# Hybrid streaming encoder on one core: the streams' RoPE scores as one single-pass product of split keys and queries

## The reference, cut to what matters

```python
def mla_attend(q_lat, q_pe, ckv, kpe, q_pos, k_pos):
    s = einsum('bqhc,bkc->bhqk', q_lat, ckv) + einsum('bqhr,bkr->bhqk', q_pe, kpe)
    s = where(mask, s * MLA_SCALE, min)
    p = softmax(s, axis=-1)
    return einsum('bhqk,bkc->bqhc', p, ckv)
```

## Time and profile before

| | |
|---|---|
| median of 3 runs | 2976.04 us |
| the runs | 2971.38, 2976.04, 2981.77 |
| the profiled execution's own time | 2976.23 us |
| its span, first to last instruction | 2974.4 us |
| mean granted TensorE clock | 0.972 |
| TensorE matmul busy | 2803.0 us (94%) |
| VectorE busy | 1292.5 us (43%) |
| ScalarE busy | 883.6 us (30%) |
| GpSimd busy | 348.3 us (12%) |

### The profile page before, as it was taken

The page is one execution under the profiler, slowest core; times in us unless marked ns, Lnnn a source line. Parts: engine busy times, 40 slices in busy tenths (PEclk is TensorE's granted clock), DMA queues, the critical chain, the costliest instruction groups (busy, mean ns, idle before and its releaser), DMA issues.

```text
span 2974.4 us, 45234 instructions
## 1 busy us (share of the span) xinstructions
PE 2803.0 (94%) x18690; PEld 2663.0 (90%) x18690; DVE 1292.5 (43%) x1803; ACT 883.6 (30%) x1158; POOL 348.3 (12%) x310
## 2 busy tenths in 40 slices
PE   6999999998988999999999999999889799999997
PEld 6999999995667999999989999989766688999997
DVE  3332334546566533333363323354475656332334
ACT  4221223316422332122342212242363234221222
POOL 0110111002121111001101001110202210100110
PEclk8999999999988999999999999999999799999998
DMA  3222224210004222222222232233000142223222
GB/s 109 76 66 85 71 61 107 67 40 7 20 17 80 58 71 74 80 72 62 82 69 71 73 83 71 62 84 88 19 3 28 45 72 57 71 68 87 71 58 76
DMA packets 367380, 190.42 MB, mean 64 GB/s; under 512 B 36421, under 2 KB 363160, under 8 KB 367262
## 3 DMA queue, kind: packets, MB, share of 16 engines
q1 hardware_dynamic: 363262, 178.30, 22.5%
q0 software_dynamic: 4000, 10.47, 1.4%
HBM read 182.81 MB, written 5.93 MB: 63 GB/s over the span
## 4 chain that ended last, share of the span: by engine, by line
PE 85%; DVE 8%; ACT 3%; issue 3%; SPq 0%; DMA 0%; ACTq 0%; DVEq 0%; POOL 0%; POOLq 0%
PE ps L582 25%; PE ps L583 24%; PE ps L584 24%; PE ps L817 2%; ACT w L1234 1%; PE ps L826 1%; DVE w L1661 1%; PE ps L877 1%; PE ps L945 1%; PE ps L859 1%; DVE y L1750 1%; PE ps L923 1%; DVE at L1932 1%; PE ps L924 1%; PE ps L618 0%
## 5 line engine op out<-in xcount | busy, mean ns | idle before, releaser
L582 PE MATMUL ps<-xh,w 128*128 128x320 f32 x3456 | 1081.8, 313 | 44.6 <-DVE xl L1729 17.6
L583 PE MATMUL ps<-xl,w 128*128 128x320 f32 x3456 | 1075.8, 311 | 0.0
L584 PE MATMUL ps<-xh,w 128*128 128x320 f32 x3456 | 1075.8, 311 | 0.0
L582 PEld LDWEIGHTS ps<-xh,w 128*128 128x128 f32 x3456 | 656.0, 190 | 55.8 <-DVE xl L1729 24.3
L583 PEld LDWEIGHTS ps<-xl,w 128*128 128x128 f32 x3456 | 656.1, 190 | 0.3
L584 PEld LDWEIGHTS ps<-xh,w 128*128 128x128 f32 x3456 | 655.8, 190 | 0.0
L1661 DVE TENSOR_TENSOR w<-raw,w 128x2048 fp32r<-128x2048 f32 x180 | 420.5, 2336 | 420.5 <-ACT w L1234 420.5
L1234 ACT ACTIVATE w<-raw 128x2048 fp32r<-128x2048 f32 x181 | 345.2, 1907 | 452.3 <-PE ps L584 437.6
L582 PE MATMUL ps<-hh,w 128*128 128x320 f32 x1408 | 437.4, 311 | 1.0 <-DVE w L1661 1.0
L584 PE MATMUL ps<-hh,w 128*128 128x320 f32 x1408 | 435.1, 309 | 0.0
L583 PE MATMUL ps<-hl,w 128*128 128x320 f32 x1408 | 435.1, 309 | 0.0
(11 more groups left out here) (347 smaller groups left out, 2737.8 us busy)
## 6 DMA issues: line engine op xcount, KB each, us to landing
raw<-in_w_ffn_in_dram SPq DMA_DIRECT2D x178, 512.0 KB
raw<-in_w_ffn_out_dram SPq DMA_DIRECT2D x64, 384.0 KB
raw<-in_w_ffn_out_dram SPq DMA_DIRECT2D x64, 320.0 KB
raw<-in_w_in_dram SPq DMA_DIRECT2D x38, 512.0 KB
raw<-in_w_out_dram SPq DMA_DIRECT2D x16, 512.0 KB
out_dram<-xio SPq DMA_DIRECT2D x5, 512.0 KB, 2.6
xio<-in_x_prompt_dram SPq DMA_DIRECT2D x1, 2048.0 KB
y<-in_cache_ckv_dram POOLq DMA_DIRECT2D x8, 256.0 KB, 3.2
```

Source lines behind the costliest of these rows:

```text
L582: pe.matmul(out, wh, xh, start=first, stop=False)
L583: pe.matmul(out, wh, xl, start=False, stop=False)
L584: return pe.matmul(out, wl, xh, start=False, stop=last)
```

## The change

The three partial products of a split RoPE score, high by high, high by low and low by high, are laid below each other in the 128 contracted rows, so that one float32r product of 512 columns replaces the float32 product of L924. Rows 0 to 31 hold the queries' high part and the keys' high part; rows 32 to 63 the queries' high and the keys' low; rows 64 to 95 the queries' low and the keys' high; rows 96 to 127 are zero. ACT writes the keys' high part twice, DVE the low part. The unsplit queries go to QRAW, in rows 32 to 63 of the scratch tile UB, and are split once per layer. KPT lies where it lay, over GB. On ACT the first exponential now stands ahead of stream 1's keys, and TensorE's first `stream_transpose` gets three spins. Two semaphores (`setup_ps`, `y_stored`) are merged into others (`xio_ps`, `ml_stored`), with the thresholds moved along.

```diff
-    QPE = tile(s_w, "qpe", [P, NSEQ, H, TS])
+    QPE = tile(s_w, "qpe", [P, NSEQ, H, TS], F32R)
-    KN = tile(s_w, "kn", [ROPE, P])
+    KN = tile(s_w, "kn", [2 * ROPE, P])
+    QRAW = UB[ROPE:2 * ROPE, :, :].rearrange("p c t -> p (c t)")[:, 0:NSEQ * P].rearrange("p (b h t) -> p b h t", b=NSEQ, h=H)
+    rope_hi, rope_lo = event("rope_hi", NSEQ + 1), event("rope_lo", NSEQ + 1)
...
 TensorE, stream_keys
             if b:
                 pe.wait_ge(*ct_sb.nth(l, b - 1))
+                pe.wait_ge(*rope_lo.nth(l, b))
...
 TensorE, stream_scores
             pe.wait_ge(*ct_sb.nth(l, b))
+            pe.wait_ge(*rope_lo.nth(l, b + 1))
...
-            qn = QPE[0:ROPE, b, :, :].rearrange("c h t -> c (h t)")
+            qn = QRAW[:, b, :, :].rearrange("c h t -> c (h t)")
             pe.matmul(PS[:, 4, :], ql, CT[:, b % 2, :], start=True, stop=False)
             pe.matmul(PS[:, 4, :], qp, KPT[:, b % 2, 0:PAST], start=False, stop=True)
...
 TensorE, stream_transpose
             if b:
                 pe.wait_ge(*spt_sb.nth(l, b - 1))
-                held(pe)
-                spin(PS[:, 2, :], 1)
+            held(pe)
+            spin(PS[:, 2, :], 1 if b else 3)
             pe.wait_ge(*sp_sb.nth(l, b))
...
 ACT, latent_queries
-                run(QPE[0:ROPE, :, h, :], PS[0:ROPE, 2, P:2 * P].rearrange("p (b t) -> p b t", t=TS), ACT.Copy)\
+                run(QRAW[:, :, h, :], PS[0:ROPE, 2, P:2 * P].rearrange("p (b t) -> p b t", t=TS), ACT.Copy)\
...
 ACT, the loop over n
+                if n == NT - 2:
+                    run(QPE[ROPE:2 * ROPE, :, :, :], QRAW, ACT.Copy)
+                    run(QPE[0:ROPE, :, :, :], QRAW, ACT.Copy).then_inc(rope_hi.sem, 1)
...
 ACT, stream_keys
+                run(KPT[0:ROPE, b % 2, 0:PAST], PS[0:ROPE, 1, :], ACT.Copy).then_inc(rope_hi.sem, 1)
                 run(CT[:, b % 2, :], PS[:, 0, :], ACT.Copy)
-                run(KPT[0:ROPE, b % 2, 0:PAST], PS[0:ROPE, 1, :], ACT.Copy).then_inc(ct_sb.sem, 1)
+                act.wait_ge(*rope_hi.nth(l, b + 1))
+                run(KPT[2 * ROPE:3 * ROPE, b % 2, 0:PAST], KPT[0:ROPE, b % 2, 0:PAST].bitcast(F32), ACT.Copy)\
+                    .then_inc(ct_sb.sem, 1)
...
 ACT, the start of the streams
             pair_output(H // 2 - 1)
+            stream_exp(0)
             stream_keys(1)
-            stream_exp(0)
             stream_transposed(0)
...
 DVE, mla
-            V.memset(QPE[ROPE:64, :, :, :], 0.0)
-            V.memset(QPE[64:P, :, :, :], 0.0)
+            V.memset(QPE[3 * ROPE:P, :, :, :].bitcast(F32), 0.0)
...
                 if n == NT - 3:
-                    V.memset(KPT[ROPE:64, :, 0:PAST], 0.0)
-                    V.memset(KPT[64:P, :, 0:PAST], 0.0)
+                    V.memset(KPT[3 * ROPE:P, :, 0:PAST].bitcast(F32), 0.0)
+            dve.wait_ge(*rope_hi.nth(l, 0))
+            V.tensor_tensor(QPE[2 * ROPE:3 * ROPE, :, :, :], QRAW, QPE[ROPE:2 * ROPE, :, :, :].bitcast(F32), ALU.subtract)\
+                .then_inc(rope_lo.sem, 1)
             for n in range(NT - 3, NT):
                 normalise(n)
+
+            def stream_rope_low(b):
+                dve.wait_ge(*rope_hi.nth(l, b + 1))
+                V.tensor_tensor(KPT[ROPE:2 * ROPE, b % 2, 0:PAST], PS[0:ROPE, 1, :],
+                                KPT[0:ROPE, b % 2, 0:PAST].bitcast(F32), ALU.subtract).then_inc(rope_lo.sem, 1)
...
             dve.wait_ge(*pn_zero.nth(l, 0))
...
+            stream_rope_low(0)
             stream_maximum(0)
             level(0)
             stream_normalise(0)
             level(1)
+            stream_rope_low(1)
             stream_maximum(1)
...
                 for k in range(early):
+                    if k == early - 1 and b + 2 < NSEQ:
+                        stream_rope_low(b + 2)
                     level(m + k)
```

More of the change, by code:

```diff
@@ L182, in encoder @@
     tile(ctx, "w_rest", [P, P * 2])
+    s_w = ExitStack()
+    KPT = tile(s_w, "kpt", [P, 2, T], F32R)
+    s_w.close()
     GB = tile(ctx, "gb", [P, 2, T])
@@ L273, in encoder @@
     s_w.close()
-    ROPET, SWAP, PAIR, KPT = UB[NOPE:P, 0, :], UB[0:QK, 1, 0:P], UB[NOPE:P, 1, P:P + ROPE], GB
+    ROPET, SWAP, PAIR = UB[NOPE:P, 0, :], UB[0:QK, 1, 0:P], UB[NOPE:P, 1, P:P + ROPE]
+    QRAW = UB[ROPE:2 * ROPE, :, :].rearrange("p c t -> p (c t)")[:, 0:NSEQ * P].rearrange("p (b h t) -> p b h t", b=NSEQ, h=H)
     SC, DROP = PB[0:NSEQ * 3, 0, :], KPER[0:MH, :]
@@ L318, in encoder @@
     setup_in = sem("setup_in")
-    setup_ps, setup_sb = sem("setup_ps"), sem("setup_sb")
+    setup_sb = sem("setup_sb")
     xio_ps, xio_sb = sem("xio_ps"), sem("xio_sb")
@@ L393, in encoder @@
     ml_stored = sem("ml_stored")
-    y_stored = sem("y_stored")
     act_chain, dve_chain, pool_chain = sem("act_chain"), sem("dve_chain"), sem("pool_chain")
@@ L570, in _ @@
             dst = O["y_prompt"][0, t * P:(t + 1) * P, :] if t < PT_ else O["y_sample"].rearrange("b t f -> (b t) f")
-            sp.dma_start(dst, XIO[:, t, :]).then_inc(y_stored, 16)
-        sp.wait_ge(y_stored, 16 * TILES)
+            sp.dma_start(dst, XIO[:, t, :]).then_inc(ml_stored, 16)
         sp.wait_ge(stored, 16 * LAYER_STORES * LAYERS)
         sp.wait_ge(cn_stored, 32 * LAYERS)
-        sp.wait_ge(ml_stored, 256 * LAYERS)
+        sp.wait_ge(ml_stored, 256 * LAYERS + 16 * TILES)
     @block.tensor
@@ L925, in stream_scores @@
             pe.matmul(PS[:, 5, 0:TS], ql, CKVT[:, TP + b * TS:TP + (b + 1) * TS], start=True, stop=False)
-            pe.matmul(PS[:, 5, 0:TS], qn, KN[:, b * TS:(b + 1) * TS], start=False, stop=True)\
+            pe.matmul(PS[:, 5, 0:TS], qn, KN[ROPE:2 * ROPE, b * TS:(b + 1) * TS], start=False, stop=True)\
                 .then_inc(ss_ps.sem, 1)
@@ L1173, in _ @@
         pe.transpose(PS[:, 0, 96:146], PROW[0:50, 1, :], IDENT[0:50, 0:50])
-        pe.matmul(PS[:, 1, 0:LAYERS * DK], ONES[0:1, :], HROW[:, :], start=True, stop=True).then_inc(setup_ps, 1)
+        pe.matmul(PS[:, 1, 0:LAYERS * DK], ONES[0:1, :], HROW[:, :], start=True, stop=True).then_inc(xio_ps, 1)
         pe.wait_ge(setup_sb, 1)
@@ L1540, in mla @@
             stream_keys(0)
-            run(KN[:, :], KPER[NOPE:QK, TP:T], ACT.Copy).then_inc(kn_sb.sem, 1)
+            run(KN[ROPE:2 * ROPE, :], KPER[NOPE:QK, TP:T], ACT.Copy).then_inc(kn_sb.sem, 1)
             pair_output(H // 2 - 1)
+            stream_exp(0)
             stream_keys(1)
-            stream_exp(0)
             stream_transposed(0)
@@ L1627, in _ @@
         for c in range(KD):
-            act.wait_ge(xio_ps, c + 1)
+            act.wait_ge(xio_ps, c + 2)
             run(X[:, c, :], psf[:, (c % 4) * 1024:(c % 4) * 1024 + T], ACT.Copy).then_inc(xio_sb, 1)
@@ L1649, in _ @@
         for t in range(TILES):
-            act.wait_ge(xio_ps, KD + t + 1)
+            act.wait_ge(xio_ps, KD + t + 2)
             run(XIO[:, t, :], psf[:, (t % 4) * 1024:(t % 4) * 1024 + D], ACT.Copy).then_inc(xio_sb, 1)
@@ L2229, in _ @@
         V.memset(HB[:, 0, 4:6], 1.0).then_inc(dve_setup, 1)
-        dve.wait_ge(setup_ps, 1)
+        dve.wait_ge(xio_ps, 1)
         V.tensor_copy(PAR[:, :], PS[:, 0, 0:PAR.shape[1]]).then_inc(dve_setup, 1)
```

## The result

The changed kernel takes 2980.62 us (median of 17 runs, 2971.28 to 2983.93), the kernel before 2974.43 in the same series (17 runs, 2970.86 to 2981.77): ratio 1.0018, 95% interval 1.0009 to 1.0026. That is 0.2% slower, less than the 0.3% that counts as a difference here. The forecast was 4.5 us less; measured are 6.2 more, and the interval takes in neither a gain nor no change. The time itself lies inside the forecast's range of 2963 to 2982.

What follows compares the result with a forecast made beforehand. TensorE's chain of waits (85%) was taken as the bound. Full-clock terms 1.45 - 4.55 + 1.5 gave -1.6 a layer, -3.2 in all; with -1.3 for the clock, -4.5 from 2976.2: 2971.5 us, range 2963 to 2982.

Steps and rivals of the forecast that it cites:

- The product: RoPE score product L924 falls from 0.86 to 0.21 us: -0.65 a stream, 10.4 over 16 streams where TensorE is the bound.
- The first exponential: From stream 0's maximum to its transposes' end, the exponential ahead of stream 1's keys shortens 5.06 to 3.8: gain 1.26.
- The handover: Prompt's attention to streams: query split delays values(31) by 2.48 and scores(0) by 3.36; half clock to about 785 adds 2.4 each layer.
- The clearing of KPT: One of two memsets ahead of maximum(30) goes, so TensorE waits less for what follows: -0.74, bounds -0.6 and -1.17.
- The pause of 0.25 behind the subtraction: DVE, ahead of normalise(29): a 0.25 pause because an output starts in other partitions, read from the pause before the memsets.
- The low parts in the streams: Streams 2 to 7: the low part on DVE between two level copies delays scores by 0.25 each, +1.5 a layer.
- Layer 0's long half clock gone: Layer 0's half-clock stretch in the streams vanishes as the 2.33 pause is filled: -6.1 us.
- Together -1.3: Clock term: layer 0's long stretch gone, -6.1, against a new half-clock stretch from values(31) in each layer, +2.4 each.
- The rivals: Four alternatives: no half clock 0.23, handover hiding itself 0.07, product no cheaper 0.06, long half clock 0.12; forecast 0.52.
- the slower rival: After the 3.0 pause at the handover, half clock lasts to about 803 in both layers: +11.3, 2987.5 us; chance 0.12.
- no half clock: No half clock anywhere after the change, despite the longer handover pause: 2965 to 2967 us; chance 0.23.

Runs made afterwards that it cites:

- e7: Changed kernel with its single-pass RoPE product issued four times per stream instead of once; 2990.49 us, ratio 1.0056.
- e6: Changed kernel with the first exponential back behind stream 1's keys and one spin ahead of the first transposes; 3016.14 us, ratio 1.0131.
- e10: e2 with the first exponential back behind stream 1's keys and one spin ahead of the first transposes; 3009.29 us, ratio 1.0127.
- e8: Changed kernel with 8 spin products added at the end of the streams in each layer; 2979.45 us, ratio 1.0018.
- e5: Changed kernel with 14 spin products in TensorE's wait ahead of the triangle's last values; 2990.43 us, ratio 1.006.
- e1: Changed kernel with DVE's subtraction for the queries' low part moved behind the last normalisations; 2973.8 us, ratio 1.0004.
- e3: Kernel before with a single-pass RoPE product of rounded operands, low parts left out; 2970.51 us, ratio 0.9984.
- e4: Kernel before with only the sooner first exponential and three spins ahead of the first transposes; 2972.86 us, ratio 0.9992.
- e9: Kernel before with the edits of e3 and e4 together, no low parts; 2972.25 us, ratio 1.0001.
- e13: e11 without any spin ahead of the streams' transposes; 2975.7 us, ratio 1.0005.
- e16: e1 with each product behind only its own wait, as in e11; 2982.67 us, ratio 1.0025.
- e11: e2 with TensorE's waits set apart, each ahead of the product that needs it; 2978.34 us, ratio 1.0024.
- e2: Changed kernel with the queries split in three lots under the triangle's steps, first keys' low part ahead of the PNEW wait; 2968.8 us, ratio 0.998.
- e14: e2 run again with nothing changed; 2971.43 us, ratio 0.9997.
- e15: e11 with three spins ahead of every stream's transposes; 2964.49 us (five runs), ratio 0.9959.
- e17: Changed kernel with three spins ahead of every stream's transposes; 2981.28 us, ratio 1.0023.
- e18: Kernel before with three spins ahead of every stream's transposes; 2980.92 us, ratio 1.002.

## Why the prediction failed, point by point

- **The product: right.** -0.65 a stream. The rule from the Trainium skill ("Perfetto Trace Analysis", Engine Utilization), read as the cost of a whole float32 product, would have had 0.21 saved (an estimate from it). From start to start 0.65 were saved, and e7's single passes cost 0.23 each, against 0.86 for the float32 product: about four times.
- **The first exponential: right in size**, 1.42 for 1.26. That it also keeps TensorE from a long half clock (e6, e10) was not foreseen.
- **The handover: mechanism right, the sum right with errors that cancel.** The forecast had +3.36 and 5.4 us of half clock from values(31) on, 3.0 of them ahead of the first score (1.3 us of time): 4.7. Measured are 4.7 and 5.0. But values(31) came 3.4 later for the forecast 2.5, and the half clock lasted 3.4 us for 5.4. The clearing of KPT did give its 0.7 (TensorE's wait for ACT ahead of step 30's transposes fell from 1.01 to 0.24), but the triangle ahead of it ran 0.9 to 1.1 longer. The forecast had no such term. 0.5 of it is the copy of the unsplit queries in its new place, in both layers; in layer 0 0.4 more fell in the first 31 us, at a lower mean clock (0.86 for 0.91 over the first 36.5), and the rest of layer 1's was not followed. ACT's two copies took 2.1 us for 1.8. The pause of 0.25 behind the subtraction did not show: normalise(29) started 0.02 behind its end. So the 0.25 ahead of the memsets can't be read as the price of an output in other partitions, as the prediction read it.
- **The low parts in the streams: sum right by luck, wrong place.** Forecast 0.25 for each of six, 1.5; measured 0.39 for stream 2, 1.29 for stream 3, none later, 1.7. The row of one middle stream was taken for all, though DVE's order is not the same in all. The period of an undisturbed stream fell by 0.49, between the product's 0.65 and the 0.4 forecast.
- **Layer 0's long half clock gone: right**, -9.3 in layer 0 against -3.7 in layer 1. So the attention in both layers, where the whole forecast of -4.5 lay, came out at -3.3.
- **The step that failed is "Together -1.3", the clock term.** It looked only at the stage that changes, and took every stage behind at its old time, without a reason. Measured there and ahead are +7.9: mLSTM 3.4, the stretch between the layers 3.6, the start 1.3, the end -0.4. For mLSTM e8 shows it to be the clock alone, and set by when the stage begins. For the stretch between, the pair of FFN windows shows half clock behind the same wait. No edit explains it: e5 with 1210.3 and e1 with 1210.4 have it as short as the kernel before, e3 and e4 with 1213.7 and 1213.8 as long as the changed one. The start took 663.5 to 666.6 in the 20 profiled executions, with nothing edited there. So 3.4 of the 7.9 are shown to come of the change, through the earlier begin of the stage. The other 4.5 may be the one execution's, and whether they stand in the medians is open.
- **The rivals.** None came true. The long half clock after the 3.0 wait, the slower rival, did not come in the changed kernel; it came in e6, where a second wait follows, in e10, where only the second is left, and in e5, e9, e13 and e16, with neither. So its condition, the length of the handover's wait, is wrong. The fast rival "no half clock" did come true for the streams themselves (0 us in both layers), but not for the handover.

**What stays open** is what sets the half clock off in the streams. Shown: layers of one execution with the same instructions differ (e9, e13, e16). Each of the 16 falls to half clock inside the streams of the profiled executions begins within a wait of TensorE of 0.91 us or more, or at most 2.1 us behind its end. In e9, e11, e13 and e16 it is always the same 0.91 or 0.92 for DVE's level copy, 16 to 17 us behind the first score, and the fall comes 1.5 to 1.8 us behind it, in five of the eight layers. In e2, e5 and twice in e6 it is the 1.29 of stream 3; in the kernel before, e3, e10 and twice in e6 it is the 2.33 or 2.96 ahead of the first transposes. This was read off afterwards, and no run tested it. But none of these waits is enough: each stands in other layers without a fall (2.33 in layer 1 of the kernel before, 1.29 in both layers of the changed kernel and of e14, 0.92 in both of e15). Three spins a stream left no fall in the streams of e15, e17 and e18. Whether the spins did that is not shown by these six layers, as e15 still has the wait of 0.92; for it speak e15's runs, whose clock is 0.971 or more in all five, while it was 0.970 or less in eleven of e11's twelve. Without any spins (e13) the median was 2975.7, not worse than e11's, so more spins is not simply better. The spins were not tried at another place. e15's five runs are few beside the twelve of e11, and a sixth of another kind can't be excluded.

## What to carry to other kernels

Price an edit at full clock and check it with one run per part; then ask separately what the granted clock does in the stages behind, because that clock was worth more here than the whole change: e14's runs at 0.967 took 11 to 18 us more than those at 0.971 to 0.976. When work is moved ahead of a handover, put it under steps where its engine is idle (e2). Giving each product only its own waits (e11) took 1.8 us off the streams at full clock, but the median kept it only with the spins of e15. And when a copy gets a new place, look at what it does to the instructions beside it. Compare the runs' clocks, not the median alone: a faster kernel whose runs fall into groups by clock has not kept its gain.

## What the chip showed that was not expected

- A program with less work for TensorE can be slower: e11 and e9 did the streams in 70 us at full clock and in up to 87 us in the other layer, and 14 spin products more in each layer (e15) made the kernel 13.9 us faster in the median, across two series.
- An ACT copy of 32x128 that writes rows 32 to 63 instead of 0 to 31 started 0.28 behind the start of the one before it instead of 0.16, that is at its end and not 0.1 ahead of it, and held the one behind it as well. That it is the rows, and not the other tile, was not tried apart.
- Half clock lasts for 34 to 41 us with TensorE busy throughout (e6, e9, e16); busy alone does not bring the clock back.
- Filling a wait with spins (e5) held the clock at that place and lost it later, 7 and 24 us of it.
- A delay of 2 us can be nearly free (e8: 0.6 and 0.4 us), because the stage behind it had 1.6 us less from half clock.
